# The opening of a two-layer transformer block rebuilt: first projections from the unnormed input, scaled behind

## The reference, cut to what matters

```python
h = rms_norm(x, g_pre_mix)                 # x * rsqrt(mean(x*x) + eps) * gain
proj = h @ w_in
sb_q, sb_k, sb_v, q_lat, kv_lat, k_rope = split(proj)
# stick-breaking attention, per head and block of 128 queries
z = (sb_q @ sb_k.T) * 64 ** -0.5           # strictly causal
log_keep = where(strict, -softplus(z), 0)
weights = exp(log_sigmoid(z) + cumsum_after(log_keep)); o_sb = weights @ sb_v
# latent attention
q  = rms_norm(q_lat, g_q_lat) @ w_q_up     # 8 heads of 64 + 32 rotary columns
kv = rms_norm(kv_lat, g_kv_lat) @ w_kv_up
q_rope, k_rope = apply_rope(..., cos(positions * inv_freq), sin(positions * inv_freq))
```

## Time and profile before

| | |
|---|---|
| median of 3 runs | 872.5 us (872.3 to 876.47) |
| the profiled execution | 875.89 us, of which its span 874.2 us |
| TensorE matmul busy | 827.0 us, 95% |
| VectorE busy | 638.9 us, 73% |
| ScalarE busy | 499.1 us, 57% |
| GpSimd busy | 314.9 us, 36% |
| DMA | 137.18 MB, mean 157 GB/s |

### The profile page before, as it was taken

The page is one execution under the profiler, slowest core; times in us unless marked ns, Lnnn a source line. Parts: engine busy times, 40 slices in busy tenths (PEclk is TensorE's granted clock), DMA queues, the critical chain, the costliest instruction groups (busy, mean ns, idle before and its releaser), DMA issues.

```text
span 874.2 us, 16984 instructions
## 1 busy us (share of the span) xinstructions
PE 827.0 (95%) x6722; PEld 790.3 (90%) x6722; DVE 638.9 (73%) x981; ACT 499.1 (57%) x914; POOL 314.9 (36%) x148
## 2 busy tenths in 40 slices
PE   3999999999999999999999789889999999999998
PEld 2998989899999999788999679778999999999998
DVE  6895773888887773768899869955765676667774
ACT  5765746755665657756767464367546544444441
POOL 2842223123333234344566533332454223322321
PEclk8999999999999999999999999999999999999999
DMA  5643223364766665352655542322454457666651
GB/s 208 250 146 135 73 97 124 98 201 147 236 219 197 195 192 169 109 180 97 203 183 180 189 126 72 98 73 73 145 186 152 145 171 227 185 192 192 193 169 49
DMA packets 57246, 137.18 MB, mean 157 GB/s; under 512 B 6352, under 2 KB 27088, under 8 KB 57168
## 3 DMA queue, kind: packets, MB, share of 16 engines
q1 hardware_dynamic: 57168, 136.11, 48.9%
HBM read 135.03 MB, written 1.05 MB: 156 GB/s over the span
## 4 chain that ended last, share of the span: by engine, by line
PE 76%; DVE 12%; ACT 6%; issue 4%; DMA 1%; SPq 0%; DVEq 0%; ACTq 0%
PE PROD L628 14%; PE PROD L629 14%; PE PROD L630 14%; PE PROD L690 3%; PE OP L628 2%; PE OP L630 2%; PE OP L629 2%; DVE wlo L1638 2%; DVE RS L1646 2%; PE TP L629 2%; PE SC L629 2%; PE TP L630 2%; PE SC L630 2%; PE TP L628 2%; PE SC L628 2%
## 5 line engine op out<-in xcount | busy, mean ns | idle before, releaser
L611 POOL TENSOR_TENSOR wlo<-raw,whi 128x1024 fp32r<-128x1024 f32 x124 | 311.5, 2519 | 538.7 <-ACT whi L1120 514.6
L628 PE MATMUL PROD<-HA,whi 128*128 128x256 f32 x1088 | 308.8, 284 | 13.9 <-DVE HA L1667 7.0
L629 PE MATMUL PROD<-HA,wlo 128*128 128x256 f32 x1088 | 303.7, 279 | 0.0
L630 PE MATMUL PROD<-HA,whi 128*128 128x256 f32 x1088 | 303.5, 279 | 0.0
L1120 ACT ACTIVATE whi<-raw 128x1024 fp32r<-128x1024 f32 x252 | 262.7, 1055 | 58.5 <-PE PROD L630 32.8
L1638 DVE TENSOR_TENSOR wlo<-raw,whi 128x1024 fp32r<-128x1024 f32 x128 | 191.4, 1497 | 82.0 <-ACT whi L1120 81.9
L628 PEld LDWEIGHTS PROD<-HA,whi 128*128 128x128 f32 x1088 | 207.0, 190 | 17.2 <-DVE HA L1667 7.7
L629 PEld LDWEIGHTS PROD<-HA,wlo 128*128 128x128 f32 x1088 | 207.1, 190 | 0.8 <-issue 0.7
L630 PEld LDWEIGHTS PROD<-HA,whi 128*128 128x128 f32 x1088 | 207.1, 190 | 0.0
L1646 DVE RECIPROCAL RS<-RTT 128x256 f32<-128x256 f32 (+2 forms) x18 | 42.8, 2380 | 17.8 <-ACT RTT L1139 17.7
L628 PE MATMUL OP<-HA,whi 128*128 128x256 f32 x192 | 53.7, 280 | 0.7 <-DVE KS L1723 0.5
(11 more groups left out here) (330 smaller groups left out, 1637.3 us busy)
## 6 DMA issues: line engine op xcount, KB each, us to landing
raw<-stream SPq DMA_DIRECT2D x197, 512.0 KB, 4.1
raw<-stream SPq DMA_DIRECT2D x144, 128.0 KB, 2.5
raw<-stream SPq DMA_DIRECT2D x28, 256.0 KB, 3.0
raw<-stream SPq DMA_DIRECT2D x4, 384.0 KB, 3.4
X<-xT SPq DMA_DIRECT2D x2, 512.0 KB, 5.5
out<-X SPq DMA_DIRECT2D x8, 128.0 KB, 2.0
KMEM<-memT SPq DMA_DIRECT2D x1, 512.0 KB, 5.2
VMEM<-memT SPq DMA_DIRECT2D x1, 512.0 KB, 6.2
```

The costliest lines, as they stand in the source:

```text
L611: nc.gpsimd.tensor_tensor(wlo[:, n % NSPLIT, :], raw[:, n % NRAW, :], whi[:, n % NSPLIT, :].bitcast(F32), ALU.subtract).then_inc(lo_pool, 1)
L628: nc.tensor.matmul(dst, wh, hi, start=start, stop=False, skip_group_check=True)
L629: nc.tensor.matmul(dst, wl, hi, start=False, stop=False, skip_group_check=True)
L630: last = nc.tensor.matmul(dst, wh, lo, start=False, stop=stop, skip_group_check=True)
```

## The change

The norm of `h1` commutes with the projection, since it is one factor per token. So the first projections now take `x` times the gain, unnormed, and their results are multiplied by the reciprocal root behind.

- Loads: the eight gain columns first, then the first half of `x`, tile 0, the second half, tile 1, positions and the other constants, tile 2 and the rest.
- ScalarE writes high parts straight from `x`, splits tiles 0 to 2, then squares, and splits 3 and 4 between; VectorE writes low parts from `x` and the low halves of tiles 0 and 1; GpSimd those of 2 to 5.
- Angles: sine and cosine side by side, 512 columns to an instruction, in PSUM (`TP` and `SC`), eleven instructions.
- The sum for `h1` comes behind `lat` 1, in `TP`; its reciprocal goes to `RSF`. VectorE takes `lat` 0 to 2 out times `RSF`, ScalarE squares the copies. `lat` 3 goes to the bank `OP` and is rotated with a table that carries the factor. The factor of `sbq` and `sbk` is put on the scores (one per key, one per query: two instructions for each pair of heads), that of `sbv` on its copy; for these, two one-column matmuls turn the factor to a column per token.
- TensorE runs 20 idle 128 x 128 x 128 float32 products before the first projection, in groups of 8, 5, 4 and 3 behind four waits.

```diff
--- before.py
+++ after.py
@@ -123,6 +123,8 @@
+    if n < NSPLIT:
+        return n < 2
@@ -149,8 +151,7 @@
-    out = [("stat", "h1")]
-    out += [("lat", m) for m in range(4)]
+    out = [("lat", 0), ("lat", 1), ("stat", "h1"), ("lat", 2), ("lat", 3)]
@@ -205,20 +206,21 @@
+IN_TP = {("stat", "h1"): 6, ("stat", "memk0"): 6, ("stat", "memk1"): 7}
...
-    elif _o in (("stat", "memk0"), ("stat", "memk1")):
-        _k, PREV[_o] = 6 + int(_o[1][-1]), None
+    elif _o in IN_TP:
+        _k, PREV[_o] = IN_TP[_o], None
...
-        _k = min(range(NBANK + (_o in FFN_OUTS)), key=lambda k: _seen[k])
+        _k = min(range(NBANK + (_o in FFN_OUTS or _o == ("lat", 3))), key=lambda k: _seen[k])
@@ -289,7 +291,7 @@
-TN0 = bases([("h1", 4), ("ql", 1), ("kvl", 1), ("mem", 4), ("xn2", 4)])
+TN0 = bases([("ql", 1), ("kvl", 1), ("mem", 4), ("xn2", 4)])
@@ -321,7 +323,7 @@
-        sb("behind_hl", [P, 64])
+        sb("behind_hl", [P, 48])
@@ -343,6 +345,7 @@
+        rtok = sb("rtok", [P, 16])
@@ -377,6 +380,8 @@
+        ANG, RT_TOK = TP[:, 512:512 + S], TP[:, 512 + S:512 + S + QT]
+        REST, WHOLE = [SC[:, 512 * i:512 * i + 512].rearrange("p (a s) -> p a s", a=2) for i in range(2)]
@@ -392,6 +397,7 @@
+        gain_in = sem("gain_in")
@@ -414,6 +420,7 @@
+        rtok_ready = sem("rtok_ready")
@@ -535,10 +542,11 @@
-            sp.dma_start(Y[:, 1, :].bitcast(I32), pos).then_inc(pos_in, 16)
-            sp.dma_start(CV[:, :], consts).then_inc(consts_in, 16)
-            for i in range(2):
+            def x_half(i):
...
+            sp.dma_start(CV[:, 0:8], consts[:, 0:8]).then_inc(gain_in, 16)
+            x_half(0)
@@ -546,7 +554,12 @@
-                if n == 6:
+                if n == 0:
+                    x_half(1)
+                elif n == 1:
+                    sp.dma_start(Y[:, 1, :].bitcast(I32), pos).then_inc(pos_in, 16)
+                    sp.dma_start(CV[:, 8:NCONST], consts[:, 8:NCONST]).then_inc(consts_in, 16)
+                elif n == 6:
@@ -717,6 +730,8 @@
+                if u == 0:
+                    pe.wait_ge(sincos, 2)
@@ -732,6 +747,8 @@
+                if u == 0:
+                    pe.wait_ge(rt_ready, RT["h1"] + 1)
@@ -745,6 +762,8 @@
+                if u == 0:
+                    wait_freed(pe, ("lat", 3))
@@ -844,11 +863,31 @@
+            def keep_busy(n):
+                for _ in range(n):
+                    nc.tensor.matmul(OP[:, 0:P], ones[:, :], ones[:, :], start=True, stop=True)
+            pe.wait_ge(pchain, 2)
+            keep_busy(8)
+            pe.wait_ge(a_hi, SP0["h1"] + 1)
+            keep_busy(5)
+            pe.wait_ge(a_hi, SP0["h1"] + 4)
+            keep_busy(4)
+            pe.wait_ge(hi_done, 1)
+            keep_busy(3)
+            fm("lat", 0, HA, SP0["h1"])
+            fm("lat", 1, HA)
+            stat("h1", [SQ[:, c, :] for c in range(8)])
+            fm("lat", 2, HA)
+            fm("lat", 3, HA)
+            fm("sbq", 0, HA)
...
-            stat("h1", [SQ[:, c, :] for c in range(8)])
-            for m in range(4):
-                fm("lat", m, HA, SP0["h1"] if m == 0 else None)
-            fm("sbq", 0, HA)
+            pe.wait_ge(rs_ready, RT["h1"] + 1)
+            for qt in range(QT):
+                last = nc.tensor.matmul(RT_TOK[:, qt:qt + 1], RSF[:, qt * P:(qt + 1) * P], ident[:, 0:1], start=True,
+                                        stop=True, skip_group_check=True)
+            last.then_inc(rtok_ready, 1)
@@ -1201,29 +1240,30 @@
-            act.wait_ge(masks, 1)
+            act.wait_ge(pchain, 10)
...
-            for c in range(8):
-                if c % 4 == 0:
-                    act.wait_ge(x_in[c // 4], 16)
-                squares("h1", c, X[:, c, :])
-            weights(1)
+            act.wait_ge(gain_in, 16)
+            for half in range(2):
+                act.wait_ge(x_in[half], 16)
+                for c in range(4 * half, 4 * half + 4):
+                    high(HA, c, X[:, c, :], CV[:, COL["g_pre_mix"] + c:COL["g_pre_mix"] + c + 1])
+                weights(1 + 2 * half)
+            for half in range(2):
+                for c in range(4 * half, 4 * half + 4):
+                    squares("h1", c, X[:, c, :])
+                weights(4 + half)
+            act.wait_ge(angles, 1)
+            nc.scalar.activation(SIN[:, :], REST[:, 0, :], ACT.Sin).then_inc(sincos, 1)
+            nc.scalar.activation(COS[:, :], REST[:, 1, :], ACT.Sin).then_inc(sincos, 1)
+            warm(ACT.Sqrt)
+            root("h1", D)
...
-            act.wait_ge(angles, 2)
-            nc.scalar.activation(SIN[:, :], SIN[:, :], ACT.Sin).then_inc(sincos, 1)
-            nc.scalar.activation(COS[:, :], COS[:, :], ACT.Sin).then_inc(sincos, 1)
-            root("h1", D)
-            normed_high(HA, "h1", 8, "g_pre_mix")
...
-            act.wait_ge(a_lo, SP0["h1"] + 8)
...
-                wait_product(act, ("lat", m))
-                src = product(("lat", m))[:, 0:S]
-                squares(None, m, src)
-                nc.scalar.activation(Y[:, 4 + m, :], src, ACT.Copy).then_inc(free(("lat", m)), 1)
+                wait_freed(act, ("lat", m))
+                squares(None, m, Y[:, 4 + m, :])
@@ -1751,38 +1791,46 @@
-            ang, turns = Y[:, 0, :], Y[:, 2, :]
+            for half in range(2):
+                for c in range(4 * half, 4 * half + 4):
+                    low(HA, "h1", c, X[:, c, :], CV[:, COL["g_pre_mix"] + c:COL["g_pre_mix"] + c + 1])
+                weights(1 + half)
...
-            link(nc.vector.tensor_copy(Y[:, 3, :], Y[:, 1, :].bitcast(I32)))
-            link(nc.vector.tensor_scalar(ang, Y[:, 3, :], CV[:, COL["freq"]:COL["freq"] + 1], None, ALU.mult))
-            for dst, quarter in ((SIN, 0.0), (COS, 0.25)):
-                link(nc.vector.tensor_scalar(turns, ang, 1 / (2 * math.pi), quarter, ALU.mult, ALU.add))
-                link(nc.vector.tensor_scalar(turns, turns, magic, None, ALU.add))
-                link(nc.vector.tensor_scalar(turns, turns, magic, None, ALU.subtract))
-                src = ang
-                for c in (c1, c2, c3):
-                    link(nc.vector.scalar_tensor_tensor(out=dst[:, :], in0=turns, scalar=-c, in1=src, op0=ALU.mult,
-                                                        op1=ALU.add))
-                    src = dst[:, :]
-                link(nc.vector.tensor_scalar(dst[:, :], dst[:, :], 2 * math.pi * quarter, 3.1415925, ALU.add, ALU.min))
-                nc.vector.tensor_scalar(dst[:, :], dst[:, :], -3.1415925, None, ALU.max).then_inc(angles, 1)
-            inverse_root("h1")
-            scaled("h1", X, 8)
-            weights(2)
-            normed_low(HA, "h1", "h1", 8, "g_pre_mix")
-            weights(NSPLIT)
+            link(nc.vector.tensor_copy(ANG, Y[:, 1, :].bitcast(I32)))
+            link(nc.vector.tensor_scalar(ANG, ANG, CV[:, COL["freq"]:COL["freq"] + 1], None, ALU.mult))
+            for i in range(2):
+                ins = nc.vector.tensor_scalar(WHOLE[:, i, :], ANG, 1 / (2 * math.pi), 0.25 * i, ALU.mult, ALU.add)
+            link(ins)
+            link(nc.vector.tensor_scalar(WHOLE, WHOLE, magic, None, ALU.add))
+            turns = Y[:, 2:4, :]
+            link(nc.vector.tensor_scalar(turns, WHOLE, magic, None, ALU.subtract))
+            src = ANG.unsqueeze(1).to_broadcast((P, 2, S))
+            for c in (c1, c2, c3):
+                link(nc.vector.scalar_tensor_tensor(out=REST, in0=turns, scalar=-c, in1=src, op0=ALU.mult,
+                                                    op1=ALU.add))
+                src = REST
+            link(nc.vector.tensor_scalar(REST[:, 1, :], REST[:, 1, :], math.pi / 2, None, ALU.add))
+            nc.vector.tensor_scalar(REST, REST, 3.1415925, -3.1415925, ALU.min, ALU.max).then_inc(angles, 1)
+            inverse_root("h1", dst=RSF)
+            for m in range(3):
+                o = ("lat", m)
+                wait_product(dve, o)
+                nc.vector.tensor_tensor(Y[:, 4 + m, :], product(o)[:, 0:S], RSF[:, :], ALU.mult).then_inc(free(o), 1)
+                ahead(o)
...
-            for m in range(3):
-                ahead(("lat", m))
+            link(nc.vector.tensor_tensor(Y[64:128, 2, :], COS[64:128, :], RSF[64:128, :], ALU.mult))
...
-            rotated(product(o)[64:128, 0:S], COS[64:128, :], KM[64:96, 0, :], Y[64:128, 0, :]).then_inc(free(o), 1)
+            rotated(product(o)[64:128, 0:S], Y[64:128, 2, :], KM[64:96, 0, :], Y[64:128, 0, :]).then_inc(free(o), 1)
...
+            dve.wait_ge(rtok_ready, 1)
+            nc.vector.tensor_scalar(rtok[:, 0:QT], RT_TOK, DH ** -0.5, None, ALU.mult)
+            link(nc.vector.tensor_copy(rtok[:, QT:2 * QT], RT_TOK))
@@ -1793,9 +1841,13 @@
-                nc.vector.tensor_scalar(Z[:, 2 * u:2 * u + 2, :],
-                                        SC[:, :].rearrange("p (h k) -> p h k", h=2)[:, :, 0:384],
-                                        DH ** -0.5, None, ALU.mult).then_inc(sb_z, 1)
+                for qt in range(QT):
```

(9 more changed lines are left out.)

## The result

The changed kernel took 887.24 us (median of 4 runs, 881.84 to 888.34), the kernel before 873.49 beside it: ratio 1.0134, interval 1.0092 to 1.0175. The forecast was 868.2 in a range of 861.5 to 873.0. So the change gained nothing; and in the profiled executions the 1.3% of the first comparison is mostly not the opening, as the next rows show.

A forecast was written before the change was run, and what follows sets the result against it. TensorE, busy 827.0 of 874.2 us, bounds the kernel, so gains lie in the opening's holes. Scores 1 come 3.6 to 4.6 us earlier, taken as 4.3 off the 872.5 median: 868.2 us, range 861.5 to 873.0.

The forecast's parts named there:

- The front: Opening: x's first half lands at 5.2 us, angles run 12.0 to 18.6, first scaled copy out at 23.5.
- VectorE is late next: VectorE behind 23.5 us: operations wait for GpSimd's tiles, so qlat's reciprocal starts at 40.7, only 4.25 us earlier.
- Sbk 0 waits for mem's root; TensorE idles there: TensorE after sbq 3: idle from 40 to 44.5 us; the clock falls, costing about 2.8 us.
- The base: Kernel before: scores 1 start at 60.20 us; profiled execution 875.9 us, gain taken off the median of 872.5.
- The rest is unchanged in number and size... at 0.: Everything after scores 1: extra operations and waits cost 0 each, at most 0.5 us together.
- A: Rival: VectorE isn't held by GpSimd's tiles, so TensorE's 8.5 to 10.5 us decides; about 863 us; chance 0.22.
- B: Rival: x lands at 5.9 us and angles take 8, first scaled copy 2.1 later; 870.3 us; chance 0.12.
- C: Rival: the hole before sbk 0 lowers the clock through sbk 3, 6.6 us slower; 879 us; chance 0.04.
- D: Rival: VectorE's PSUM angle operations also wait for GpSimd, some 8 us late; 876 us; chance 0.04.
- E: Rival: the hole only moves from 14-20 to 40-45 us; no gain, 872.5 within 1.5; chance 0.08.
- the prediction's last sign: The prediction is wrong altogether if TensorE after 60 us is slower than before by more than 1 us.

The follow-up runs named there:

- e5: e1 with VectorE reordered: COS sign ahead of h1's reciprocal, lat 3's rotation ahead of tile 8's low half; 872.79 us, ratio 0.9948.
- e1: The changed kernel with lat 3 put into bank OP instead of bank 0; 877.0 us, ratio 1.0005 to the kernel before.
- e8: The kernel before plus a one-column bf16 matmul ahead of FFN 1's third projection and FFN 2's second; 880.35 us, ratio 1.0067.
- e12: e8 with the first added matmul moved ahead of the fourth projection of FFN 1; 881.2 us, ratio 1.0070 to the kernel before.
- e9: The changed kernel with the same two added matmuls as e8; 873.46 us, ratio 0.9980 to the kernel before.
- e13: e9 with the first added matmul moved ahead of the fourth projection of FFN 1; 872.84 us, ratio 0.9949 to the kernel before.
- p1: The changed kernel with a one-column float32 matmul added at ten places in each FFN; 884.16 us, ratio 1.0071 to the kernel before.
- p2: The changed kernel with float32 or bf16 matmuls of 1, 32 or 128 columns added at ten places in each FFN; 880.14 us, one run.
- p3: The same program as p2, run for a second profile; 879.62 us, one run.
- a2: The changed kernel, unaltered, run again; 878.75 us against 878.65 for the kernel before, ratio 1.0006.
- e7: e5 without the 20 idle products and their waits; 874.32 us, ratio 0.9996 to the kernel before.
- e10: e5 with the same two added matmuls as e8; 865.99 us, ratio 0.9895 to the kernel before.
- e11: e10 with eleven more such matmuls ahead of projections in other stages; 866.11 us, ratio 0.9902 to the kernel before.
- b2: The kernel before, unaltered, run again for a second profile; 878.52 us, one run.
- e2: The changed kernel with SBUF addresses of all tensors as in the kernel before; 873.07 us, ratio 0.9946 to the kernel before.

## Why the prediction was wrong

Point by point.

- *The front.* Right in the end, but x's first half came late: ScalarE's first high part starts at 6.10, released by that transfer, where I had 5.2 and an upper bound of 5.9. High parts and tiles 0 and 1 ran 0.9 late with it, and the angles started 0.65 late (12.65 for 12.0). From there the durations were right: angles, Sin, root and first scaled copy all ended within 0.7 us of the forecast.
- *VectorE is late next.* Right: its operations wait for GpSimd's tiles one by one, the reciprocal of qlat starts at 40.69 (40.7), and e5 shows that the order makes it so (37.1).
- *Sbk 0 waits for mem's root; TensorE idles there.* This failed for the changed kernel. I took lat 3 to be in `OP`, as the diff reads, and didn't work the planner's tie through. In bank 0 it blocks the qlat sum by a wait that stands in no term of the sum (lat 3's bank is there only as "met long before", at 0): TensorE idles 4.19 us at 33.1, the clock falls (0.53 in 35 to 40), and the third sbq projection, which I had starting at 34.5, starts at 44.3, hardly before the old 45.0. Scores 1 start at 59.91 instead of 55.6. e1 puts the bank right, and 55.37 comes out.
- *The base.* My numbers of before had a turn of 2.2 us in the angles that its second profile doesn't have (scores 1 at 57.83). Against that one e1 gains 2.5 up to scores 1, not 4.8, and the changed kernel loses 2.1 (0.7 in its own second profile, 58.50). Over the profiles with an unaltered opening, before's FFN 1 starts at 162.5, 160.1, 160.2 (e8) and 160.3 (e12), the changed kernel's at 163.7, 160.8, 162.1 (e9), 162.5 (e13), 162.8 (p1), 162.4 (p2) and 161.9 (p3): 1.5 later in the mean. The opening as changed is a small loss, not a gain of 4.3. All that lies outside the two FFNs takes 497.8 us in the mean of those four profiles and 497.7 in that of the seven: the change is worth nothing, as a2's ratio of 1.0006 says. In e1 it takes 493.9 (one profile), in e5, e7, e10 and e11 490.3 in the mean. The median of 872.5 that I took the gain off, from 3 runs, was low as well: beside the later runs before's median is 875.3 to 879.1.
- *"The rest is unchanged in number and size... at 0."* Unchanged in number; not in size. This is the step that put the time outside the range, whose upper end lies 14.2 us below the measured median: the two FFNs of the profiled run took 13.9 us more, by a matmul pace 4% slower. I had every matmul of one form at one price; the earlier trace rows show nothing of it, though means from 276 to 285 ns for one form stand on the page. Part of this is luck and not the change: b2, the kernel before, has a slow FFN 1 as well.
- *Rivals.* A happened once, in e2. B's late x came (6.10, B had 5.9), but its chain was not 2.1 late, only some 0.5: the angles took the forecast time. C's hole and low clock came, at another place. D didn't: the fused angle operations took 0.70 beside GpSimd. E, the hole is only moved, is the nearest to what the opening did. No rival had the FFNs in it; the prediction's last sign, TensorE slower after 60 us by more than 1 us, is what came.

Open: what decides the pace. Addresses, count of instructions ahead and the banks (the FFNs' banks come out in the same order in both kernels) don't decide it alone. Whether the changed program gets the slow one more often isn't settled; so neither is how much of the first 1.3% belongs to it. For it: FFN 1 starts slow in 10 of 11 profiles of the changed program and its variants in which no matmul is added directly behind memk's sums, against 2 of 5 of the program before and its variants. Against it: the medians of a2, equal in 12 and 29 runs.

## What to carry to other kernels

Work a planner's output through for the changed input, ties too, before costing a step by it. Where two engines share a resource by turns, put the short operations into time in which the other idles: moving them gave what the rebuilding had not. Profile a second run of the kernel before, and take the base from many runs, before a gain is worked out from its rows. Compare medians of many runs on more than one chip, and count matmuls per stretch, before a per cent is put down to an edit.
